# A two-layer attention trunk: the B heads' turn on VectorE and ScalarE in another order

## The reference, cut to what matters

```python
# layer 0: out_a = forgetting attention (A), out_b = sliding window (B)
x = x + concat(out_a, out_b) @ w_out        # then an MLP; layer 1 has heads C and D
# B, for each of 8 heads, blocks of 128 queries, 256 keys (two blocks), window 128:
logits = q @ k.T * d ** -0.5 + bias          # masked outside the window
p = softmax(concat(logits, sink))[..., :-1]  # the sink is one more logit of the head
out = p @ v
```

## Time and profile before

| what | value |
|---|---|
| median of 3 runs | 1159.1 us (1159.02 to 1159.28) |
| profiled execution, own time | 1159.08 us |
| its span, first to last instruction | 1157.3 us |
| granted TensorE clock, mean | 0.997 of full speed |
| busy, TensorE / VectorE / ScalarE / GpSimd | 97% / 76% / 53% / 34% |

### The profile page before, as it was taken

How to read it: one execution, slowest core, us unless ns; L and a number is a source line. 1 busy time by engine, 2 the same in 40 slices (tenths; PEclk the granted TensorE clock), 3 DMA queues, 4 the chain that set the end, 5 groups by cost and what they waited for, 6 DMA issues and landing times.

```text
span 1157.3 us, 16571 instructions
## 1 busy us (share of the span) xinstructions
PE 1118.3 (97%) x6045; PEld 944.5 (82%) x6045; DVE 879.2 (76%) x1484; ACT 614.9 (53%) x1093; POOL 388.1 (34%) x313
## 2 busy tenths in 40 slices
PE   6999998999999999999999999999999999999996
PEld 4788887788988989989977778888888888888885
DVE  5876778678778778668768999656778678787686
ACT  6577677545344344254566367864554453453443
POOL 2444333452131131140165556435521221311400
PEclk9999999999999999999999999999999999999999
DMA  4332342432341421522222100214422423315212
GB/s 150 92 111 84 99 121 62 146 116 67 108 130 55 160 84 48 181 73 63 92 55 73 37 1 20 65 46 148 126 73 69 154 69 136 102 52 182 72 37 91
DMA packets 142226, 105.55 MB, mean 91 GB/s; under 512 B 9078, under 2 KB 122017, under 8 KB 142162
## 3 DMA queue, kind: packets, MB, share of 16 engines
q1 hardware_dynamic: 140892, 104.61, 29.5%
q10 hardware_dynamic: 1270, 0.13, 0.1%
HBM read 102.56 MB, written 6.35 MB: 94 GB/s over the span
## 4 chain that ended last, share of the span: by engine, by line
PE 77%; DVE 14%; ACT 5%; issue 3%; DMA 1%; POOL 1%; SPq 0%; ACTq 0%; DVEq 0%
PE bank L811 24%; PE bank L813 23%; PE bank L812 23%; ACT probs L1557 2%; PE bank L1019 1%; DVE probT_l L2015 1%; DVE score L2484 1%; DVE best L2480 1%; ACT ur L1311 1%; PE bank L1021 1%; PE bank L1031 1%; PE bank L1032 1%; DVE bank L2363 1%; ACT wh L1311 1%; DVE xhl L2086 1%
## 5 line engine op out<-in xcount | busy, mean ns | idle before, releaser
L1823 POOL TENSOR_TENSOR wl<-raw,wh 128x512 fp32r<-128x512 f32 x213 | 288.6, 1378 | 599.0 <-ACT wh L1311 579.7
L811 PE MATMUL bank<-ur,wh 128*128 128x512 f32 (+1 forms) x624 | 237.9, 381 | 1.0 <-POOL wl L1823 0.9
L813 PE MATMUL bank<-ur,wl 128*128 128x512 f32 (+1 forms) x624 | 236.2, 378 | 0.0
L812 PE MATMUL bank<-ur,wh 128*128 128x512 f32 x560 | 218.0, 389 | 0.0
L1311 ACT ACTIVATE wh<-raw 128x1024 fp32r<-128x1024 f32 x107 | 111.9, 1053 | 128.0 <-PE bank L813 126.4
L811 PEld LDWEIGHTS bank<-ur,wh 128*128 128x128 f32 x624 | 117.4, 188 | 24.5 <-issue 3.4
L813 PEld LDWEIGHTS bank<-ur,wl 128*128 128x128 f32 x624 | 117.4, 188 | 22.0
L812 PE MATMUL bank<-xhl,wh 128*128 128x512 f32 (+2 forms) x360 | 134.4, 373 | 0.0
L811 PE MATMUL bank<-xhl,wh 128*128 128x512 f32 (+1 forms) x296 | 120.9, 409 | 5.7 <-DVE xhl L2086 4.2
L811 PE MATMUL bank<-ur 128*128 128x256 f32 (+3 forms) x352 | 117.5, 334 | 6.6 <-ACT probs L1557 2.6
L812 PEld LDWEIGHTS bank<-ur,wh 128*128 128x128 f32 x560 | 105.2, 188 | 21.8 <-issue 0.5
(11 more groups left out here) (291 smaller groups left out, 2511.8 us busy)
## 6 DMA issues: line engine op xcount, KB each, us to landing
raw<-in_w_mlp SPq DMA_DIRECT2D x64, 512.0 KB, 4.0
raw<-in_w_in_e SPq DMA_DIRECT2D x18, 512.0 KB, 3.7
probs<-in_w_mlp SPq DMA_DIRECT2D x16, 512.0 KB, 4.6
rstd_qk<-in_w_mlp SPq DMA_DIRECT2D x16, 512.0 KB, 3.9
sq<-in_w_mlp SPq DMA_DIRECT2D x16, 512.0 KB, 4.8
raw<-in_w_in_o SPq DMA_DIRECT2D x10, 512.0 KB, 3.8
raw<-in_w_out_e SPq DMA_DIRECT2D x8, 512.0 KB, 3.8
score<-in_w_mlp SPq DMA_DIRECT2D x8, 512.0 KB, 6.2
```

The costliest lines, as they stand in the source:

```text
L811: mm(dst, lhs[0], rhs[0], start=start, stop=False, skip_group_check=not check)
L812: mm(dst, lhs[0], rhs[1], start=False, stop=False, skip_group_check=not check)
L813: return mm(dst, lhs[1], rhs[0], start=False, stop=stop, skip_group_check=not check)
L1823: return nc.gpsimd.tensor_tensor(dst, a, b, ALU.subtract)
```

## The change

VectorE's turn of a B step becomes: normalise head s+1, low parts of head s, maxima of head s+2, sum of the halves of head s-1. The normalise of head 9 moves from the end of step 7 to the start of step 8. On ScalarE the rounding of the probabilities goes ahead of the output half, and the rounding of the output goes behind the exponentials. The A heads' steps keep their order; no instruction is added or taken away.

```diff
--- before.py
+++ after.py
@@ -1605,19 +1605,19 @@
 
             def first_step(s):
 
+                if NH <= s:
+                    probs_hi(s, range(2))
                 if 1 <= s:
                     output_half(s - 1)
-                if 0 <= s:
+                if 0 <= s < NH:
                     probs_hi(s, range(2))
                 placed_before(s, (0,))
                 if 0 <= s < NH:
                     probs_hi(s, (2,))
                 placed_before(s, (1,))
-                if NH <= s:
-                    output_hi(s - 1)
                 if s + 2 < 2 * NH:
                     exponentials(s + 2)
-                if 1 <= s < NH:
+                if 1 <= s:
                     output_hi(s - 1)
                 for n in slabs_of(s):
                     split_slab(n + 2)
@@ -2410,15 +2410,18 @@
 
             def first_step(s):
 
-                if 1 <= s:
+                if NH <= s:
+                    if s + 1 < 2 * NH:
+                        normalise(s + 1)
+                    probs_lo(s, range(2))
+                    if s + 2 < 2 * NH:
+                        maxima(s + 2)
                     outputs_summed(s - 1)
-                if NH <= s and s + 2 < 2 * NH:
-                    maxima(s + 2)
-                if 0 <= s:
-                    probs_lo(s, range(2))
-                if NH <= s and s + 2 < 2 * NH:
-                    normalise(s + 2)
-                if s < NH:
+                else:
+                    if 1 <= s:
+                        outputs_summed(s - 1)
+                    if 0 <= s:
+                        probs_lo(s, range(2))
                     if 0 <= s:
                         probs_lo(s, (2,))
                     maxima(s + 2)
@@ -2431,8 +2434,6 @@
                     take_slab(n, HD ** -0.5 if EVEN[n][0][0] == "q" else 1.0)
                     if n in V_INSIDE:
                         projected(placed(n) - 1, EVEN[n][0], n)
-                if s == NH - 1:
-                    normalise(NH + 1)
 
             def heads(first, last, steps):
                 for s in steps:
```

## The result

| kernel | median of the device time | ratio to before, 95% interval |
|---|---|---|
| before | 1159.02 us (5 runs) | |
| changed | 1165.08 us (5 runs, 1164.75 to 1166.04) | 1.0053 (1.0042 to 1.0064) |

A forecast was written before the change was run, and what follows sets the result against it. TensorE, busy 97% of 1157.3 us, bounds the kernel; in the B heads it follows VectorE, which rings with ScalarE. Longer rings 2.7 plus the GpSimd meeting 1.8 make 4.5 us over 1159.1: 1163.6, range 1160.1 to 1165.8.

The forecast's parts named there:

- The wait isn't removed but moved: VectorE would still wait for the exponentials, now at its normalise, 0.7 to 0.8 us, longer than before.
- The ring per turn, 5.71 instead of 5.31: VectorE and ScalarE's loop of normalise, low parts, maxima, exponentials: each undisturbed turn costs 0.40 us more.
- The second ring: Loop of values, turning, ScalarE's rounding, low parts, maxima and sum through TensorE: 5.75 us, just as long.
- Two turns with the spare split, 6.1; the one with qb3, 6.32: Turns 10 to 11 and 12 to 13 delayed by ScalarE's weight split; step 11 adds VectorE's query slab split.
- The tail from the maxima of 15 to values(15), 10.68: End of the B heads: was 9.47 us, now 10.68, late by another 1.2.
- The sum of the rings, 2.7: Lag of the B heads' stretch at values(15) from longer turns and tail: 2.5 us, taken as 2.7.
- The meeting with GpSimd, 1.77: Normalise of head 10 runs beside GpSimd's split and is held up 1.77 us, as measured at head 0.
- Sum: 2.7 + 1.8 = 4.5 us: Total loss from longer rings (2.7) and VectorE meeting GpSimd (1.8), giving 1163.6 us.
- its own course of events: Main case, meeting costs near what head 0 shows: 1163.6 us, range 1162.6 to 1164.8, chance 0.50.
- rival (b): The meeting of VectorE and GpSimd costs up to 3.8 us, three GpSimd instructions each blocking: 1165.6, chance 0.12.
- The rivals on the other side: Lag swallowed behind the heads or second ring absent: 1159.1 to 1160.3, chance 0.10; exponentials' wait gone: 1156.7, chance 0.08.
- The start of values(9), foretold for no earlier than 171.5: Sign on TensorE in step 9: the prediction is wrong if values(9) starts before 171.5.

The follow-up runs named there:

- the run with the sum ahead of the maxima: Changed kernel with GpSimd's step 8 split waiting for head 10's normalise, plus VectorE summing the output's halves before the maxima: 1164.2 us.
- Moving the split: Changed kernel with GpSimd's step 8 split waiting for head 10's normalise, plus ScalarE's spare weight splits (steps 10, 12) put before the exponentials: 1160.7 us.
- With GpSimd waiting: Changed kernel, but GpSimd's split at step 8 waits until head 10 is normalised: 1162.1 us.
- the run with the filler: Changed kernel with 12 TensorE products that nobody reads ahead of values(9) in step 9: 1163.9 us.
- the run with ScalarE's part alone: Kernel before with only ScalarE's order changed, VectorE keeping its old turn: 1165.4 us.
- the run with VectorE's part alone: Only VectorE's turn changed, ScalarE keeping the order of the kernel before: 1172.4 us.

## Why the prediction was right, point by point

*The wait isn't removed but moved.* Right. Foretold: 0.6 to 0.8 us in steps 10, 11, 13 and 14; the trace has four waits of 0.60.

*The ring per turn, 5.71 instead of 5.31.* The number is near, 5.77 or 5.78 where nothing else disturbs it, but the ring that it was worked out for is not the one that sets it. The ring through the exponentials is about 5.5 (5.54 in the run with the sum ahead of the maxima, without the sum), nearly 0.2 shorter than forecast. The second ring, through values and the turning, for which the prediction had 5.75, "just as long", holds VectorE up for another 0.25 us at the low parts, and so it is the one that paces the turn. The size came out right by the second ring.

*Two turns with the spare split, 6.1; the one with qb3, 6.32.* Right in kind, 0.15 short: 6.24, 6.25 and 6.38. Moving the split took 0.46 back each time.

*The tail from the maxima of 15 to values(15), 10.68.* With GpSimd waiting, 203.77 - 192.85 = 10.92.

*The sum of the rings, 2.7.* Measured 2.95. The prediction's layout has values(15) 38.15 us behind ScalarE's split, measured 38.57: the way to the maxima of head 11 was put 0.22 too long (3.23 for 3.01), the four turns 0.40 and the tail 0.24 too short.

*The meeting with GpSimd, 1.77, "with some multiplications over a microsecond".* Right in place and cause, sized 0.3 too low: the stretch shows 2.07. The price was taken from head 0, where the two met less completely. In the trace of the kernel before, one of its multiplications took 1.47 us instead of 0.42, held up for most of a GpSimd instruction. The first caught only the end of one (0.63 instead of 0.29), and the last met a shorter one of 0.99 us (0.84 instead of 0.48). In step 9 two multiplications were held up for about 1.0 us each.

*"Sum: 2.7 + 1.8 = 4.5 us."* This is the step that fell short, as it left a term out: in the profiled execution 2.95 + 2.07 + 1.25 = 6.27. The 1.25 is TensorE's clock. The prediction counted that a later low part makes TensorE stand still, and took the work behind the standstill at its usual durations. The rings and the meeting make 5.0, and the run with the filler, which has both and kept its clock, lies 4.9 over before. For the rest of the 6.1, a little over 1 us, the low clock is the likely cause; it is shown for one execution of five, and what made it fall stays open.

*The time.* It lies in the range, but above the 1162.6 to 1164.8 that the prediction gave its own course of events, and near the 1165.6 of rival (b), three GpSimd instructions each holding one up. That was not what happened: the normalise lost 2.1 us and not 3.8, so (b) would have been near the time by the wrong road.

*The rivals on the other side.* The wait at the first MLP that would swallow the lag wasn't there: 470.9 us behind values(15), in the second layer, the changed kernel still has all of the lag. The exponentials took no less time than before.

*The start of values(9), foretold for no earlier than 171.5.* Right, and later still against the slab. It starts at 171.89, 7.53 us after ScalarE's split at 164.36; before, it was 171.04 - 166.23 = 4.81.

## What to carry to other kernels

Two engines that wait for each other in turn form a ring, and its length is read off by walking it once: what lies between an instruction and the one that it waits for is hidden, the rest is paid in each turn. Rotating the order moves work onto the ring or off it; on the ring through the exponentials the low parts (1.06 us) went on and the sum (0.73) came off, and a wait of 0.3 us became one of 0.6. Walk every ring that the new order closes: here the one through TensorE was the longer, and it showed in the second, shorter wait of VectorE's turn and not in the first, longer one. Before a bottleneck is moved earlier in time, look at what then runs beside it on another engine, and at how long TensorE will stand: it may pay for the standstill twice. Where a clock can fall in one execution and not in the next, one profile of each kernel does not tell what brings it down.

## What the runs showed of the hardware

The fall of TensorE's clock was not expected. Around the end of a standstill of 2.95 us the granted clock fell to 0.50, 1.2 GHz, for some 3 us, and came back while TensorE worked without a gap; it cost 1.25 us. In other runs it fell after standstills of 2.33 and 2.30 us (the sum ahead of the maxima), and in the run with ScalarE's part alone after two waits of only 0.91 and 0.67 us close together. Against that, the run with VectorE's part alone stood for 2.96 us in front of the same values(9) and kept its full clock. The second layer says the same: in all nine profiles TensorE stands there once for 2.59 us, and the clock fell within 2 us of its end in seven of them, but not in the kernel before nor in the run with the sum ahead of the maxima. From values(15) to the end of the span, where all nine run the same code, those two took 955.4 and 955.5 us, the other seven 956.3 to 958.1. So a part of the spread between single runs is this fall, the same standstill does not always bring it, and its length alone does not decide; what does stays open.

The meeting on SBUF: beside GpSimd's subtractions VectorE's first two multiplications ran as always (0.29 and 0.35 us), and the other two took 1.38 and 1.39 us instead of 0.35, each as long as one GpSimd instruction; GpSimd's first took 1.45 instead of 1.27. The two took turns, an instruction at a time. The Trainium skill calls the shared port pair an exclusive lock, held for the whole instruction (SBUF — State Buffer, section on its two separate sides). The trace agrees; here two of four instructions met it, and so the cost was 2.07 us and not the 3.8 that the prediction drew from this rule.
